# Ten units of an input projection as Strassen products in a hybrid decoder layer

## The chip, the core and the metric

The kernel runs on one core of one Trainium2 chip. The metric is device time in microseconds (us) of one launch. Five engines with a queue of their own work side by side: TensorE (PE) does matmuls out of SBUF into PSUM, VectorE (DVE) and ScalarE (ACT) do elementwise work, GpSimd (POOL) and SyncE (SP) here mostly issue DMAs. They meet on semaphores.

## What is computed

One decoder layer in fp32 for a prompt of 256 tokens and 8 samples of 8 tokens, 320 tokens in all. The part that the change touches is the first projection and its gates:

```
u = rmsnorm(x, norm1, NORM_EPS) @ w_in
qa, ka, va, qb, kb, vb, g_low, r_b, g_a, g_b = jnp.split(u, offsets, axis=-1)
...
ob = rmsnorm(ob, gla_norm, NORM_EPS).reshape(*x.shape[:-1], B_WIDTH) * jax.nn.silu(r_b)
merged = jax.nn.sigmoid(g_a) * (oa @ w_a) + jax.nn.sigmoid(g_b) * (ob @ w_b)
h = x + merged @ w_o
return h + moe(rmsnorm(h, norm2, NORM_EPS), w_router, b_router, w1, b1, w2, b2)
```

oa is sliding-window attention with a sink per head, ob gated linear attention (GLA) in chunks. r_b has 512 columns, g_a and g_b 1024 each; each column is a sum over 1024 model dimensions. The MoE has 32 experts, whose fp32 weights are most of the 440 MB that the kernel reads.

## The kernel before

**Memory.** `ring` is 20 slots of 2048 fp32 per partition (1 MB each). In the first part its slots hold weight units, small operands and results by name: `region_g` (slots 14 to 17) rbT, rsT, gaT and gbT, `late` (4, 5) the cached keys and values and the attention scores, `low` (0 to 3) the GLA operands and states. Later five rooms of four slots take expert weights as they come free. `xnT` holds the normed input transposed, 8 blocks of 128 dimensions by 320 tokens.

**Projection.** w_in is read in units of 256 columns, 15 of them (`W_UNITS`); six ring slots take them in turn (`load_unit`, L378), each loaded again when the unit in it is used up. `project(n)` (L639 to L691) forms tile n of `TILE_ORDER` in PSUM bank n % 3: first k, v, q and the GLA operands (tiles 0 to 15), then four r_b, eight g_a and eight g_b tiles (16 to 35). Each of these twenty is 8 matmuls of a 128x128 weight block with 320 token columns (L689), and a unit makes two tiles. ACT copies every tile out of its bank (`evacuate`, L1338); g_b tiles go through a sigmoid on the way (L1368), r_b and g_a through one later (`gates_early`, L1414).

**Order around the change.** It is written out by hand. PE runs its twenty tiles as s = 0 to 19 and does, behind tile s, the steps of the table `between`: for attention step t of 0 to 4 `scores(t)` (L719), then `turn_probs(t)` (transposes, L743), then `attend(t)` (L756); from s = 12 on the GLA steps `decays`, `turn_keys` (L792), `state_steps(w)` (L800), `sample_reads` and `gla_out`. Among them: s = 4 has turn_probs(0) and scores(1), s = 5 attend(0), s = 6 turn_probs(1) and scores(2), s = 15 state_steps(0) and turn_keys(1), s = 16 state_steps(1) and turn_keys(2), s = 17 state_steps(2) and the prompt's gla_out. ACT has the like table `after`: gla_prep, gla_exps, the exponentials `exps(t)` (L1398), the copies `probs(t)`. DVE's order is a straight list: `softmax_max(t)` (L1705 to L1718) waits for scores(t); `softmax_norm(t)` (L1729 to L1731) waits for exps(t) and releases turn_probs(t); `attended(t)` (L1738) copies attend(t) out. `gla_operands` (L1797 to L1811) stands between softmax_max(1) and attended(0). `mask_keys(t)` (L1765, L1768) waits for turn_keys(t) and releases a later state_steps; `step_states(w)` (L1781 to L1787) takes state_steps(w) out of PSUM. Each engine does its list in order, so what stands behind a waiting instruction waits too.

**After the tiles** PE does `branch` (L906): eight groups of matmuls oa @ w_a, eight ob @ w_b, DVE merging them with the gates. Then `project_h` (merged @ w_o), the router, and the experts.

**SP's order.** Units, then w_a (when tile 29 is done), w_b (after attend(4)), w_o (after all tiles), x again, then expert weights, room by room, each waiting for the event that frees its slots.

**POOL** clears pads, issues the small loads and the stores of new keys and values (L577, L579) and the loads of b1 (L583).

Of the kernel before, what the change touches and what calls it, by code (L numbers as in the profile page):

```python
# [54 lines left out]
FIRST_SLOT, STREAM_SLOTS = 6, 6  # L55
# [6 lines left out]
    + [("vb", t) for t in range(3)] + [("rb", j) for j in range(4)] \  # L62
    + [("ga", j) for j in range(8)] + [("gb", j) for j in range(8)]
FIRST_RB = 16
# [19 lines left out]
def unit_done(m):  # L84

    last = [("va", 2), ("q", 3), ("q", 3), ("qb", 1), ("kb", 1), ("vb", 2), ("vb", 2)]
    return tiles_done(*last[m]) if m < len(last) else FIRST_RB + 2 * (m - 6)

# [71 lines left out]
def layer(nc: bass.Bass, x_prompt, x_sample, cache_k, cache_v, state_gla, norm1, w_in, q_norm, k_norm,  # L160
          sinks, w_gk, b_gk, gla_norm, w_a, w_b, w_o, norm2, w_router, b_router, w1, b1, w2, b2, consts,
          y_prompt, y_sample, k_prompt, v_prompt, s_prompt, k_sample, v_sample, s_sample):
    with ExitStack() as ctx:
# [134 lines left out]
        unit_in = [sem(f"unit_in{m}") for m in range(STREAM_SLOTS)]  # L298
# [6 lines left out]
        pj_ready, pj_freed = sem("pj_ready"), sem("pj_freed")  # L305
        sq_ready, var_ready, qk_rstd, qk_done = (sem(n) for n in ("sq_ready", "var_ready", "qk_rstd", "qk_done"))
# [32 lines left out]
        def slot_of(m):  # L339
            return FIRST_SLOT + m % STREAM_SLOTS  # L340

        def unit(m):
            return ring[:, slot_of(m), :].rearrange("p (k c) -> p k c", k=KD)

# [28 lines left out]
        def _(sp):  # L373
# [4 lines left out]
            def load_unit(m):  # L378
                c = W_UNITS[m]
                sp.dma_start(unit(m), w_in[0, :, c:c + UNIT].rearrange("(k p) c -> p k c", p=P)  # L380
                             ).then_inc(unit_in[m % STREAM_SLOTS], 16)

            for m in range(STREAM_SLOTS):
# [3 lines left out]
            for m in range(STREAM_SLOTS, NU):  # L387
                sp.wait_ge(pj_ready, unit_done(m - STREAM_SLOTS))
                load_unit(m)
                if m == STREAM_SLOTS + 2:  # L390
# [3 lines left out]
            sp.wait_ge(pj_ready, unit_done(13))  # L394
            for g in range(KVH):
                sp.dma_start(wa_sb[HD * g:HD * g + HD, :, :],
                             w_a[0, 256 * g:256 * g + 256, :].rearrange("(j d) c -> d j c", d=HD)).then_inc(wa_in, 16)
            sp.wait_ge(n_ready, use(N_USES, "attend4"))
            sp.dma_start(wb_sb, w_b[0].rearrange("(h v) c -> v h c", v=GDV)).then_inc(wb_in, 16)
            sp.wait_ge(pj_ready, len(TILE_ORDER))  # L400
# [56 lines left out]
            load_half(1, 0)  # L457
            load_half(2, 1)
# [79 lines left out]
        def _(pool):  # L538
# [37 lines left out]
            pool.wait_ge(n_freed, use(N_USES, "keys"))  # L576
            pool.dma_start(k_prompt[0, 0].rearrange("w g d -> w (g d)"), kTok[:, 0, :]).then_inc(stores, 16)  # L577
            for b in range(NSEQ):
                pool.dma_start(k_sample[0, b, P - TSEQ:P].rearrange("w g d -> w (g d)"),  # L579
                               kTok[TSEQ * b:TSEQ * b + TSEQ, 1, :]).then_inc(stores, 16)  # L580

            for g in range(4):
                pool.dma_start(sig_flat.rearrange("p (e x) -> p e x", e=EXPERTS)[:, 8 * g:8 * g + 8, :],  # L583
                               b1[0, 8 * g:8 * g + 8, :].rearrange("e (p x) -> p e x", p=P)).then_inc(b1_in, 16)
# [10 lines left out]
        def _(pe):  # L595
# [38 lines left out]
            def need_unit(m):  # L634
                if m >= unit_at[0]:
                    pe.wait_ge(unit_in[m % STREAM_SLOTS], 16 * (m // STREAM_SLOTS + 1))
                    unit_at[0] = m + 1

            def project(n):  # L639
# [43 lines left out]
                m = {"k": 0, "qb": 3, "kb": 4, "rb": 7, "ga": 9, "gb": 13}[kind] + j // 2  # L683
# [7 lines left out]
                mm.then_inc(pj_ready, 1)  # L691

# [174 lines left out]
            for n in range(FIRST_RB):  # L867
# [26 lines left out]
            for s in range(20):  # L894
                project(FIRST_RB + s)
                for step in between.get(s, ()):
                    step()


            def branch(w_sb, operand, m, u):  # L900
                if u < 3:
                    pe.wait_ge(pj_freed, len(TILE_ORDER))
# [7 lines left out]
            pe.wait_ge(wa_in, 32)  # L910
# [393 lines left out]
        def _(act):  # L1304
# [33 lines left out]
            def evacuate(n):  # L1338
# [22 lines left out]
                elif kind == "glow":  # L1361
                    nc.scalar.copy(glT[:, :], ps[:, n % 3, 0:T]).then_inc(pj_freed, 1)
                elif kind == "rb":
# [745 lines left out]
```

## Time and profile before

| what | us |
|---|---|
| three timed runs: median (lowest to highest) | 1196.55 (1196.08 to 1202.88) |
| the profiled execution | 1200.83 |
| its span, first to last instruction | 1198.6 |
| PE busy in the span | 1156.9 |
| DVE, ACT, POOL busy | 325.8, 170.0, 28.2 |

The profile is of one execution. An engine is busy while an instruction of it is in progress; matmuls are pipelined, so the sum of their lengths is more than the time they take, and what a stream of them costs is read from the spacing. Waiting is shown as the idle time before an instruction, with what ended it. One matmul of the code is two instructions of the profile.

### The profile page before, as it was taken

Reading aid. Unit: us, or ns where it says so; the run is one execution under the profiler, and the core shown is the slowest. Engines: PE = TensorE matmul, PEld = TensorE weight load, DVE = VectorE, ACT = ScalarE, POOL = GpSimd, SP = SyncE. Lnnn points to the kernel's source line nnn. Section 1 sums busy time; section 2 is a strip of 40 time slices with the busy share of each in tenths; the row PEclk is TensorE's granted clock in tenths of the full one; section 3 lists DMA queues with packets and bytes.
Section 4 is the critical chain, followed back from the end, with each engine's and each line's share of the span. In section 5 each row is a group of like instructions: output and inputs, shape, how many; then the busy total and the mean of one; then the engine's idle time right before and its main releaser. Section 6 shows DMA issues by size and latency. Waiting matters only on the chain.

```text
span 1198.6 us, 13581 instructions
## 1 busy us (share of the span) xinstructions
PE 1156.9 (97%) x5929; PEld 552.7 (46%) x5929; DVE 325.8 (27%) x675; ACT 170.0 (14%) x310; POOL 28.2 (2%) x53
## 2 busy tenths in 40 slices
PE   9999999999999999999999999999999999899998
PEld 7676677645344343434344343434343434343433
DVE  3405434624223221212223221222221212121222
ACT  2114322013111010111011010101010101010111
POOL 4102000000000000000000000000000000000000
PEclk9999999999999999999999999999999999999999
DMA  9744153975999999999999999999999999999996
GB/s 303 222 129 118 36 141 133 409 330 198 384 421 428 429 435 431 428 434 432 424 433 436 426 433 433 430 431 430 433 426 435 433 426 431 434 429 425 428 428 243
DMA packets 45054, 439.99 MB, mean 367 GB/s; under 512 B 3646, under 2 KB 21408, under 8 KB 29616
## 3 DMA queue, kind: packets, MB, share of 16 engines
q1 hardware_dynamic: 42864, 434.19, 87.2%
q0 software_dynamic: 1888, 4.10, 1.2%
q8 instruction: 49, 0.80, 0.3%
q10 hardware_dynamic: 240, 0.79, 0.2%
q14 instruction: 13, 0.11, 0.0%
HBM read 436.38 MB, written 3.67 MB: 367 GB/s over the span
## 4 chain that ended last, share of the span: by engine, by line
PE 66%; DMA 30%; DVE 1%; issue 1%; ACT 1%; DVEq 0%
DMA ring<-in_w 30%; PE ps L1125 21%; PE ps L1183 13%; PE ps L689 9%; PE ps L1200 4%; PE ps L906 3%; PE ps L1003 3%; PE ps L926 2%; PE ps L679 1%; PE ps L656 1%; PE ps L1140 1%; ACT xnT L1540 1%; PE ps L1011 1%; PE ps L1152 1%; PE ps L930 1%
## 5 line engine op out<-in xcount | busy, mean ns | idle before, releaser
L1125 PE MATMUL ps<-ring,hnT 128*64 128x512 f32 x2032 | 446.9, 596 | 11.3 <-DMA ring<-in_w 10.6
L1125 PEld LDWEIGHTS ps<-ring,hnT 128*64 128x64 f32 x2032 | 142.9, 137 | 299.8 <-issue 279.6
L1183 PE MATMUL ps<-ring,xnT 128*64 128x512 f32 x992 | 222.6, 601 | 17.6 <-DMA ring<-in_w 17.6
L1183 PEld LDWEIGHTS ps<-ring,xnT 128*64 128x64 f32 x992 | 75.7, 138 | 160.2 <-issue 157.4
L2009 DVE TENSOR_TENSOR xnT<-ps,b1T 128x512 f32<-128x512 f32 x32 | 22.1, 692 | 445.2 <-PE ps L1140 445.2
L689 PE MATMUL ps<-xnT,ring 128*128 128x320 f32 x400 | 114.3, 441 | 1.1 <-DVE xnT L1633 1.1
L1527 ACT COPY hnT<-ps 128x1024 f32<-128x1024 f32 x32 | 32.4, 1012 | 516.0 <-PE ps L1125 516.0
L2030 DVE TENSOR_TENSOR acc<-acc,ps 128x1024 f32<-128x1024 f32 x32 | 38.9, 1218 | 210.1 <-PE ps L1200 210.1
L689 PEld LDWEIGHTS ps<-xnT,ring 128*128 128x128 f32 x400 | 75.5, 192 | 33.8 <-issue 3.0
L1200 PE MATMUL ps<-xnT,cst 128*128 128x512 f32 (+3 forms) x192 | 79.3, 617 | 1.5
L1003 PE MATMUL ps<-cst,region 128*128 128x128 f32 x512 | 63.2, 282 | 0.7 <-issue 0.7
L1003 PEld LDWEIGHTS ps<-cst,region 128*128 128x128 f32 x512 | 59.8, 195 | 2.7 <-issue 0.9
L1539 ACT COPY xnT<-ps 64x512 f32<-64x512 f32 x31 | 17.9, 578 | 245.7 <-PE ps L1183 245.7
L1200 PEld LDWEIGHTS ps<-xnT,cst 128*128 128x128 f32 (+3 forms) x192 | 24.9, 170 | 44.6 <-issue 40.1
L1140 PEld LDWEIGHTS ps<-cst,hnT 128*128 128x128 f32 x256 | 33.3, 210 | 25.9 <-issue 25.2
L1140 PE MATMUL ps<-cst,hnT 128*128 128x128 f32 x256 | 39.3, 297 | 0.6 <-ACT hnT L1527 0.6
L926 PE MATMUL ps<-ring,xnT 128*128 128x512 f32 x64 | 29.8, 603 | 0.0
L2001 DVE TENSOR_TENSOR hnT<-ps,n_cols 128x512 f32<-128x512 f32 x32 | 22.0, 688 | 15.9 <-PE ps L1003 15.9
L1533 ACT ACTIVATE sig<-xnT 128x512 f32<-128x512 f32 x32 | 20.2, 630 | 27.4 <-DVE xnT L2013 27.4
L1988 DVE TENSOR_SCALAR cst<-cst,place,gates 128x64 f32<-128x64 f32 (+1 forms) x96 | 22.6, 303 | 0.0
L2020 DVE SCALAR_TENSOR_TENSOR hnT<-hnT,xnT 128x512 f32<-128x512 f32 x32 | 22.2, 693 | 1.1
L2025 DVE TENSOR_TENSOR xnT<-hnT,sig 128x512 f32<-128x512 f32 x32 | 22.1, 692 | 1.1
(291 smaller groups left out, 666.4 us busy)
## 6 DMA issues: line engine op xcount, KB each, us to landing
ring<-in_w SPq DMA_DIRECT2D x71, 4096.0 KB, 39.7
ring<-in_w SPq DMA_DIRECT2D x46, 2048.0 KB, 17.6
ring<-in_w_in SPq DMA_DIRECT2D x17, 1024.0 KB, 7.7
ring<-in_w_o SPq DMA_DIRECT2D x2, 2048.0 KB, 14.3
ring<-in_w SPq DMA_DIRECT2D x8, 512.0 KB, 23.0
ring<-in_w_a SPq DMA_DIRECT2D x2, 1024.0 KB, 9.6
ring<-in_w_b SPq DMA_DIRECT2D x1, 2048.0 KB, 15.6
ring<-in_w SPq DMA_DIRECT2D x2, 1024.0 KB, 11.6
```

The source lines that it names most:

```text
L689: mm = pe.matmul(ps[:, bank, 0:T], unit(m)[:, k, c:c + P], xnT[:, k, :], start=(k == 0), stop=(k == KD - 1))
L906: mm = pe.matmul(ps[:, u % 3, 0:T], w_sb[:, k, P * m:P * m + P], operand[:, k, :], start=(k == 0), stop=(k == 3))
L926: mm = pe.matmul(ps[:, (XB, VB_)[t] + c, :], xnT[:, k, t0:t0 + r], wo_sb[c][:, k, :], start=(k == 0), stop=(k == KD - 1), skip_group_check ...
L1003: mm = pe.matmul(ps[:, XB + half, P * k:P * k + P], hn[:, t, at:at + P], pick[:, t, :], start=False, stop=last and k == 3, skip_group_chec ...
L1125: mm = pe.matmul(ps[o:o + 64, q // 2, into].rearrange("p (j x) -> p j x", x=4), stationary, columns[:, q], start=(at == 0), stop=(at == KD ...
L1140: mm = pe.transpose(ps[:, 2 + gl, o:o + P], u_sb[:, q, 2 * r + gl:2 * r + gl + 509:4], ident)
L1183: mm = pe.matmul(ps[64 * c:64 * c + 64, 6, :], hT[:, which, order_of(f), :], ring[:, slot, D * (f % 2) + 512 * c:D * (f % 2) + 512 * c + 512],
L1200: mm = pe.matmul(out, lhsT, rhs[half], start=True, stop=True)
L1527: nc.scalar.copy(u_sb[:, :, :], ps[:, 0:2, :]).then_inc(u_copied, 1)
L1988: last = dve.tensor_scalar(gpick[0:r, t, SLOTS * which:SLOTS * (which + 1)], const("slot", r), place[0:r, t, bass.ds(e + which, 1)], gates ...
L2020: dve.scalar_tensor_tensor(lin, lin, 1.0, glu, ALU.add, ALU.mult).then_inc(prod_ready, 1)
L2030: dve.tensor_tensor(acc[:, t, :], acc[:, t, :], ps[:, bank:bank + 2, :].rearrange("p a b -> p (a b)"), ALU.add).then_inc(comb_added, 1)
```

## The change

The ten r_b, g_a and g_b units (u = 0 to 9, 256 columns each) are formed by Strassen's scheme (in Winograd's form). The unit's weights are cut into blocks (i, j): column half i, half j of the 1024 dimensions; `xnT` into blocks of 512 dimensions and 160 tokens. Seven products of half size replace eight: `product(u, i)` is 4 matmuls of a 128x128 block with 160 columns. Three products share a PSUM bank (a group), and ACT copies a group to SBUF at once (`copy_group`). The weight sums of a unit, four additions or subtractions of 512 elements, each waiting for the one before, are done by POOL (`weight_sums`); the four sums of the input blocks once by DVE; and DVE puts the seven products of a unit together in four instructions (`fast_sums`), at places written into its list. The g_b sigmoids move behind that (`gate_b`). Between the fourth and the fifth product of a unit, and behind the seventh, stand the steps that stood behind its two tiles.

The ring is laid out anew: the first seven units have slots of their own, the ten others take slots 8, 6 and 7 in turn, sums go to 9 and 10, the input's sums to 11, products to 19 and the ends of 17 and 18. w_a is loaded later, in two halves, and one expert half waits for the last fast_sums. POOL's stores of keys and loads of b1 now come in pieces between the sums.

```
-            for n in range(FIRST_RB):
+            for n in range(len(TILE_ORDER)):
                 project(n)
...
-            for s in range(20):
-                project(FIRST_RB + s)
-                for step in between.get(s, ()):
+            for u in range(FAST_UNITS):
+                for i in range(4):
+                    product(u, i)
+                for step in between.get(2 * u, ()):
+                    step()
+                for i in range(4, PRODUCTS):
+                    product(u, i)
+                for step in between.get(2 * u + 1, ()):
                     step()
```

PE, a product:

```
+            def product(u, i):
+                at = PRODUCTS * u + i
+                group, part = divmod(at, GROUP_OF)
+                if part == 0:
+                    if group < 3:
+                        pe.wait_ge(pj_freed, len(TILE_ORDER) - 2 + group)
+                    else:
+                        pe.wait_ge(group_copied, group - 2)
...
+                elif i == 2:
+                    pe.wait_ge(halves_ready, 1)
+                    pe.wait_ge(sum_ready, 4 * u + 2)
+                    w, x = sum_w(u, 2), sum_x(2)
...
+                for k in range(4):
+                    mm = pe.matmul(ps[:, (group + 1) % 3, HALF_T * part:HALF_T * part + HALF_T], w[:, k, :], x[:, k, :],
+                                   start=(k == 0), stop=(k == 3), skip_group_check=True)
+                mm.then_inc(product_ready, 1)
```

POOL, the sums of a unit, and what stands between them:

```
+            def weight_sums(u):
+                m = PLAIN_UNITS + u
+                pool.wait_ge(unit_in[m % UNIT_SEMS], 16 * (m // UNIT_SEMS + 1))
+                if u >= 2:
+                    pool.wait_ge(product_ready, PRODUCTS * (u - 1))
...
+                pool.tensor_tensor(sum_w(u, 1), block_w(u, 2, 1), block_w(u, 2, 2), ALU.add).then_inc(sum_ready, 1)
+                pool.wait_ge(sum_ready, 4 * u + 1)
+                pool.tensor_tensor(sum_w(u, 2), sum_w(u, 1), block_w(u, 1, 1), ALU.subtract).then_inc(sum_ready, 1)
...
+            for u in range(FAST_UNITS):
+                weight_sums(u)
+                if u == 2:
+                    store_keys(0, 3)
...
+                elif u in (5, 6):
+                    load_b1(2 * (u - 5), 2 * (u - 4))
```

DVE, the sums of the products, and their places:

```
+            def fast_sums(u):
+                out = fast_out(u)
+                pairs = [out[:, 0:320], out[:, 160:480]]
...
+                dve.wait_ge(group_copied, (PRODUCTS * u + PRODUCTS - 1) // GROUP_OF + 1)
+                link(dve.tensor_tensor(two(pairs[0]), two(products(u, 1, 2)), wide(products(u, 0).unsqueeze(1), [P, 2, HALF_T]), ALU.add))
+                link(dve.tensor_tensor(two(products(u, 0, 2)), two(products(u, 3, 2)), wide(out[:, 160:320].unsqueeze(1), [P, 2, HALF_T]), ALU.add))
+                dve.tensor_tensor(pairs[1], products(u, 5, 2), products(u, 0, 2), ALU.add)
+                dve.tensor_tensor(out[:, 480:640], products(u, 1), products(u, 3), ALU.add).then_inc(out_ready, 1)
...
             for s in range(4):
                 softmax_norm(s)
+                if s == 0:
+                    fast_sums(0)
                 softmax_max(s + 1)
                 if s == 0:
                     gla_operands()
+                fast_sums(s + 1)
                 attended(s)
...
             step_states(1)
+            fast_sums(7)
             mask_keys(2)
             step_states(2)
+            fast_sums(8)
```

DVE between the end of gla_operands and the probabilities of attention step 1; before, the last operand (L1811) is followed by the copy of attend(0) and softmax_norm(1):

```order
L1808 TENSOR_TENSOR region<-ring 64x4x16 x2
L1811 TENSOR_TENSOR ring<-ring 128x640
L1738 COPY hnT<-ps 128x2x128
L1729 TENSOR_TENSOR small<-small 128x4
L1730 RECIPROCAL small<-small 128x4
L1731 TENSOR_TENSOR ring<-ring,small 128x4x128
```

Now, with the lines of the changed kernel (L1974 is the last operand, L1901 the copy, L1892 to L1894 softmax_norm):

```order
L1971 TENSOR_TENSOR region<-ring 64x4x16 x2
L1974 TENSOR_TENSOR ring<-ring 128x640
L1817 TENSOR_TENSOR ring<-ring 128x320
L1818 TENSOR_TENSOR ring<-ring 128x320
L1819 TENSOR_TENSOR ring<-ring 128x320
L1820 TENSOR_TENSOR ring<-ring 128x160
L1901 COPY hnT<-ps 128x2x128
L1892 TENSOR_TENSOR small<-small 128x4
L1893 RECIPROCAL small<-small 128x4
L1894 TENSOR_TENSOR ring<-ring,small 128x4x128
```

The four instructions of fast_sums(1) have come between the operands and softmax_norm(1).

DVE between step_states(1) (L1783, eight instructions) and step_states(2) (L1787), with mask_keys(2) (L1765) between them, before:

```order
L1768 TENSOR_TENSOR region<-ps,cst 128x512
L1783 SCALAR_TENSOR_TENSOR ring<-ring,dec,ps 128x128 x8
L1765 TENSOR_TENSOR region<-ps,cst 64x1024
L1787 SCALAR_TENSOR_TENSOR ring<-acc,dec,ps 128x128 x16
L1832 TENSOR_TENSOR ring<-ring 128x1280
```

Now (L1946 is step_states(1), L1928 mask_keys(2), L1950 step_states(2)):

```order
L1946 SCALAR_TENSOR_TENSOR ring<-ring,dec,ps 128x128 x8
L1817 TENSOR_TENSOR ring<-ring 128x320
L1818 TENSOR_TENSOR ring<-ring 128x320
L1819 TENSOR_TENSOR ring<-ring 128x320
L1820 TENSOR_TENSOR ring<-ring 128x160
L1928 TENSOR_TENSOR region<-ps,cst 64x1024
L1950 SCALAR_TENSOR_TENSOR ring<-acc,dec,ps 128x128 x8
```

fast_sums(7) has come ahead of the mask.

## Rows read from the trace of the kernel before

**Rows 1.** The page: span, chain by engine, and the issues of weight units.

```profile
span 1198.6 us, 13581 instructions
...
PE 66%; DMA 30%; DVE 1%; issue 1%; ACT 1%; DVEq 0%
...
ring<-in_w_in SPq DMA_DIRECT2D x17, 1024.0 KB, 7.7
```

**Rows 2.** Busy time by stage; columns PE, PEld, DVE, ACT, POOL, PEclk, DMA share, GB/s.

```profile
81.00:118.00 37.00, 36.74 (x162) 25.46 (x161) 17.30 (x45) 17.45 (x40) 8.23 (x13) 1.00 0.51 153
118.00:200.00 82.00, 82.00 (x620) 58.94 (x617) 29.31 (x72) 21.19 (x52) 1.91 (x2) 1.00 0.25 71
...
237.00:289.00 52.00, 49.66 (x234) 26.42 (x236) 15.79 (x52) 12.68 (x28) 0.00 (x0) 0.97 0.69 285
289.00:640.00 351.00, 349.73 (x1767) 142.48 (x1765) 88.43 (x181) 39.39 (x58) 0.53 (x1) 1.00 0.99 419
640.00:1173.00 533.00, 503.24 (x2480) 206.73 (x2478) 120.24 (x233) 55.70 (x83) 0.00 (x0) 0.99 1.00 430
```

**Rows 3.** PE's groups by line and shape, 81 to 200 us: the twenty tiles.

```profile
L689 PE MATMUL ps<-xnT,ring 128*128 128x320 f32 x320 | 90.5, 437 | 0.0
```

**Rows 4.** The chain in order of time: start us, us, what.

```profile
49.12 12.92 PE ps L689 x48
...
63.26 14.01 PE ps L656 x64
...
183.18 1.51 PE ps L856 x14
```

**Rows 5.** DVE in order of time, 101 to 117 us.

```profile
106.75 0.76 DVE L1705 SCALAR_TENSOR_TENSOR ring<-ps,cst 128x256 f32<-128x256 f32 x2 [4.32 <-PE ps L727]
...
108.60 0.17 DVE L1797 COPY dec<-ring 128x16 f32<-128x16 f32 x1
...
114.23 0.83 DVE L1811 TENSOR_TENSOR ring<-ring 128x640 f32<-128x640 f32 x1
114.97 0.42 DVE L1738 COPY hnT<-ps 128x256 f32<-128x256 f32 x1
...
115.71 0.69 DVE L1731 TENSOR_TENSOR ring<-ring,small 128x512 f32<-128x512 f32 x1
```

**Rows 6.** Who PE waited for, 81 to 240 us: us, times, longest.

```profile
PE ps L750 <- DVE ring L1731: 0.3, 1, 0.3
```

**Rows 7.** DVE's groups by line and shape, 86 to 117 and 200 to 222 us.

```profile
L1686 DVE TENSOR_TENSOR ring<-ring 128x128 f32<-128x128 f32 x2 | 0.5, 284 | 0.0
...
L1844 DVE TENSOR_TENSOR region<-region,xnT 128x320 f32<-128x320 f32 x4 | 1.8, 442 | 0.0
```

**Rows 8.** DVE, then PE, in order of time, 174 to 182 us.

```profile
176.48 2.53 DVE L1783 SCALAR_TENSOR_TENSOR ring<-ring,dec,ps 128x128 f32<-128x128 f32 x8 [2.58 <-PE ps L812]
178.93 1.21 DVE L1765 TENSOR_TENSOR region<-ps,cst 64x1024 f32<-64x1024 f32 x1
...
176.59 4.47 PE L689 MATMUL ps<-xnT,ring 128*128 128x320 f32 x16
180.99 1.10 PE L812 MATMUL ps<-ring,region 32*64 32x128 f32 x32
```

**Rows 9.** POOL's groups by line and shape, and DVE's slowest group.

```profile
L579 POOL DMA_DIRECT2D out<-hnT x8 | 4.1, 518 | 0.0
...
L543 POOL MEMSET ring<- 128x256 f32 x1 | 0.3, 311 | 0.0
...
L1646 DVE RECIPROCAL acc<-acc 128x320 f32<-128x320 f32 x5 | 10.8, 2153 | 0.2
```

**Rows 10.** The chain late in the kernel, and one stretch by stage.

```profile
677.25 7.10 PE ps L1183 x32
...
736.25 8.72 PE ps L1183 x32
...
736.20:739.60 3.40, 3.35 (x8) 1.13 (x10) 0.00 (x0) 0.00 (x0) 0.00 (x0) 0.51 0.96 414
```

More of the change, by code:

```diff
@@ L386, in _ @@
                     sp.dma_start(cst[:, 2 * P:NCONST], consts[:, 2 * P:NCONST]).then_inc(consts_in, 16)
[L387 to L390, printed above, removed]
+            sp.wait_ge(pj_ready, unit_done(0))
+            load_unit(PLAIN_UNITS - 1)
+            for u, before in enumerate((2, 4, 5)):
+                sp.wait_ge(pj_ready, unit_done(before))
+                load_unit(PLAIN_UNITS + u)
+                if u == 1:
                     sp.wait_ge(qk_done, 5)
@@ new lines, in store_keys, with load_b1 @@
+            def store_keys(first, end):
+                pool.wait_ge(n_freed, use(N_USES, "keys"))
+                if first == 0:
+                    pool.dma_start(k_prompt[0, 0].rearrange("w g d -> w (g d)"), kTok[:, 0, :]).then_inc(stores, 16)
+                for b in range(first, end):
+                    pool.dma_start(k_sample[0, b, P - TSEQ:P].rearrange("w g d -> w (g d)"),
+                                   kTok[TSEQ * b:TSEQ * b + TSEQ, 1, :]).then_inc(stores, 16)
+            def load_b1(first, end):
+                for g in range(first, end):
+                    pool.dma_start(sig_flat.rearrange("p (e x) -> p e x", e=EXPERTS)[:, 8 * g:8 * g + 8, :],
+                                   b1[0, 8 * g:8 * g + 8, :].rearrange("e (p x) -> p e x", p=P)).then_inc(b1_in, 16)
@@ L1360, in evacuate, with copy_group, gate_b @@
                     nc.scalar.copy(kbT[:, j, :], src).then_inc(pj_freed, 1)
-                elif kind == "glow":
+                else:
                     nc.scalar.copy(glT[:, :], ps[:, n % 3, 0:T]).then_inc(pj_freed, 1)
-                elif kind == "rb":
-                    nc.scalar.copy(rbT[:, j, :], src).then_inc(pj_freed, 1)
-                elif kind == "ga":
-                    nc.scalar.copy(gaT[:, j, :], src).then_inc(pj_freed, 1)
-                else:
-                    nc.scalar.activation(gbT[:, j, :], src, ACT.Sigmoid).then_inc(pj_freed, 1)
+            def copy_group(group):
+                first, end = GROUP_OF * group, min(GROUP_OF * group + GROUP_OF, ALL_PRODUCTS)
+                act.wait_ge(product_ready, end)
+                latest = (end - 1) // PRODUCTS
+                if latest >= 2:
+                    act.wait_ge(out_ready, latest - 1)
+                at = first
+                while at < end:
+                    u, i = divmod(at, PRODUCTS)
+                    n = 1
+                    while at + n < end and i + n < PRODUCTS and product_at(u, i + n) == product_at(u, i) + HALF_T * n:
+                        n += 1
+                    part = at - first
+                    out = nc.scalar.copy(products(u, i, n), ps[:, (group + 1) % 3, HALF_T * part:HALF_T * (part + n)])
+                    at += n
+                out.then_inc(group_copied, 1)
+            def gate_b(v):
+                act.wait_ge(out_ready, 7 + v)
+                nc.scalar.activation(gbT[:, 2 * v:2 * v + 2, :], gbT[:, 2 * v:2 * v + 2, :], ACT.Sigmoid).then_inc(gb_ready, 1)
             def root(j):
@@ L1437, in gla_sample_out @@
                 out.then_inc(vw_freed, 1)
-            for n in range(FIRST_RB):
+            for n in range(len(TILE_ORDER)):
                 evacuate(n)
@@ L1821, in _ @@
             mask_decays_prompt()
+            fast_sums(5)
             attended(4)
@@ L1824, in _ @@
             mask_keys(0)
+            fast_sums(6)
             step_states(0)
```

132 lines of the change are left out of this document (101 added, 31 removed).

## Prediction

> **What bounds the kernel now.** I read the page's head and chain first, then the busy time by stage, then PE's chain in order of time, and last what DVE does between two attention steps. The span is 1198.6 us and the chain is PE for 66% of it and DMA for 30% [rows 1]; a reader should ask which of the two rules which stage. The table by stage says it [rows 2]. From 81 to 200 us PE is busy without a gap (36.74 of 37.00, 82.00 of 82.00) while DMA is at 51% and 25%: this stretch, in which the twenty r_b and gate tiles stand between the attention and recurrence steps, is PE's. From 289 us to the end DMA is at 0.99 to 1.00 and 419 to 430 GB/s: the expert weights set the pace. Between them, 237 to 289 us, DMA has only 0.69, so the ring is full and waits for PE to free rooms. A front part that ends x us earlier therefore starts the weight stream x us earlier, and all of x reaches the end. What the change is worth is decided between 81 and 200 us.
>
> **PE work.** The twenty tiles are 320 instructions of 320 columns, 90.5 us as the profile counts them [rows 3]; the count is two per matmul in the code. What one costs is its spacing, from the chain [rows 4]: 48 of them in a row take 12.92 us, 0.2692 each, over three tiles whose waits were already met, so a met wait costs nothing. 64 of 256 columns take 14.01, 0.219 each. 160 columns have no row. Half of 0.2692 is 0.135; a line through 0.219 and 0.2692 gives 0.143, but the 0.219 holds a change of shape. Weight loads set a floor: instructions of only 64 columns behind a full 128x128 load still take 1.51/14 = 0.108. 0.135 is above it, so columns decide; I take 0.136. A product is 4 matmuls, 8 instructions, 1.09 us; a unit of seven is 7.62 against two tiles of 16 x 0.2692 = 4.31, 8.61. That is 1.0 us a unit, 10.0 for ten; with 0.143 it would be 6.0. The steps between stay, so the changes of shape cost what they did.
>
> **What is late next: DVE before turn_probs(1).** PE waits for DVE exactly once in this stretch, 0.3 us, at the transposes of the second attention step [rows 6]. So DVE's chain there had no slack left: from the end of scores(1) it does softmax_max(1) (106.75), gla_operands (108.60 to about 115.1), the copy of attend(0) and softmax_norm(1), ending at 115.71 + 0.69 = 116.40 [rows 5]. The change puts fast_sums(1) into it, behind gla_operands. One fast_sums is three instructions of 320 elements with both inputs in SBUF, 0.44 each, and one of 160, between 0.28 (128 elements) and 0.44, say 0.3 [rows 7]: 1.6 us. fast_sums(0) fits into the idle 4.3 us before 106.75. scores(1) ends 2 x 1.0 us earlier (units 0 and 1; four products, 4.35, cost the same as one tile, 4.31). So turn_probs(1) can start 2.0 - 1.6 = 0.4 us earlier than before, though PE has by then saved more: the first three and a half units yield 0.4 us, and PE idles 0.3 + 1.6 + 1.0 = 2.9 us there, the 1.0 because three products (3.26) stand where a tile (4.31) stood. Behind it the last three products of unit 3 and six units yield 1.05 + 6.0 = 7.05. In the later attention steps fast_sums lies beside ACT's exponentials, and I cost it at nothing; without that cover it is 1.6 us a step.
>
> **And before state_steps(2).** state_steps(2) needs mask_keys(2). Before, DVE did step_states(1) from 176.48 for 2.53 us and then the mask, to 180.14; PE arrived at 180.99, 0.85 late enough [rows 8]. Now fast_sums(7) stands ahead of that mask (+1.6), and PE arrives 1.05 earlier, having three products instead of a tile: 1.6 + 1.05 - 0.85 = 1.8 us lost. fast_sums(8) and (9) lie beside gla_out and the branch matmuls; the extra sigmoids on ACT too. I cost the end at nothing; 0 to 1.6 us if that cover fails.
>
> **POOL.** Forty additions of 512 elements are new; before, POOL did only memsets and DMA issues. A memset of 256 columns takes 0.311 us, so 512 written columns about 0.62; the slowest DVE row, a reciprocal of 320 elements at 2.153, would make 3.4 [rows 9]. I take 1.2, twice the memset, as two inputs are read: 4.8 us a unit, plus up to 4 DMA issues of 0.52. They have from the end of unit u-2 to the third product of unit u, a unit (119/10, less 1) and 2.2 us more: some 13. So as latency they are hidden up to about 2.7 us each. A weight unit lands in 7.7 us [rows 1], requested three units ahead: hidden.
>
> Whether POOL's reads hinder DVE no row shows. About seven of the twelve additions for units 2 to 4 fall where DVE works, with two SBUF inputs, on the chain to turn_probs(1): lower end 0, upper end 7 x 1.2 = 8.4 us. I take the middle, 4.2, since only about half of DVE's instructions there read two SBUF tensors, and a POOL instruction that starts beside another costs nothing.
>
> The Trainium skill speaks against this part of the change: "SBUF — State Buffer", section "Who interferes with whom", has a DVE instruction with two SBUF inputs and a GpSimd instruction that reads SBUF exclude each other for the whole instruction; by it alone the term would lie at its upper end. No row of this trace has the two side by side.
>
> **The clock.** PE's idle time at turn_probs(1) becomes 2.9 + 4.2 = 7.1 us. Late in the kernel waits under 3 us were at times followed by a stretch at half clock: the 32 matmuls at 736.25 took 8.72 us instead of 7.10, and the granted clock was 0.51, the 1.2 GHz level [rows 10]. One such fall: +1.6.
>
> **The sum**, against the profiled execution (1200.83 us, the span and 2.2 around it): -0.4 - 7.05 + 1.8 = -5.65 without POOL's part; + 4.2 + 1.6 gives +0.15. The median of the runs shown, 1196.55, is 4.3 below the profiled execution; the differences are the same for both, so the forecast is 1196.7, in round 1197: no change that counts. About 1% (12 us) is what a measurement of this kernel tells from no change. Its own range is 1193 to 1202.
>
> **Rivals.**
> *POOL does not hinder DVE.* Then -5.65: 1191, without a clock fall, up to 1192.5 with one. For it: DVE's instructions kept their lengths while POOL issued DMAs; against: POOL read no SBUF tensor then. Chance 0.29.
> *Strict turns, slower.* Each POOL addition stands in DVE's way and DVE never goes twice in a row. Then 8.4 at turn_probs(1), and in the next three attention steps four additions fall between softmax_max and softmax_norm: 4 x 1.2 + fast_sums 1.6 + softmax_norm at double width some 1.6 are 8.0. PE's seven products and the attend step take about 8.5 less softmax_max, 1.9 for the width of [rows 5] and about 3 for the double: 5.5 of room, so 2.5 us each, less in the last: 6 in all. -5.65 + 8.4 + 6 + 1.6 = +10.3: 1207. With additions of 1.6 us it is 11.2 + 10.8, +18: 1215; from about 1.3 us on it decides for slower by over 1%. Against: most of POOL's work could as well fall into DVE's idle time, over half of the stretch [rows 2]. Chance 0.25, half of that beyond 1%.
> The price of an addition by the skill alone: "GPSIMD Engine Reference", section "Elementwise — side-by-side cycle accounting", has 4497 ns for 2048 fp32 elements, an estimate of 1.1 us for 512; by it this rival would give 1206.
> *The sums come late.* Above 2.7 us an addition PE waits for sum_ready in each of eight units: at 3.4, 4 x 0.7 = 2.8 us each, +22 and more: 1219. Chance 0.04.
> *All ten us are kept* (DVE is quicker than its rows): 1186.6. The 0.3 us wait speaks against it: no slack to use. Chance 0.03.
>
> **How the numbers follow.** Forecast 0.39, the rivals 0.29, 0.25, 0.04, 0.03. The range must take in POOL-free (1191, with a margin of 3) and strict turns at the price I took (1207, margin 4): 1188 to 1211. That leaves out long additions, late sums and the full gain, some 0.17. Faster by over 1% would be under 1184.6, more than PE can save unless something unseen helps: 0.02. Slower by over 1%, above 1208.5: half of strict turns and late sums, 0.15. The same: 0.83.
>
> **What would show it.** Products at 0.136 us spacing, 7.6 us a unit, show the first step right. PE's wait for DVE at turn_probs(1) should grow from 0.3 to between 3 and 11 us: at 3 POOL is harmless, at 7 my middle holds, above 10 with further waits of 2 us at turn_probs(2) to (4) it is strict turns. A wait of about 1.8 us at state_steps(2) should be new. DVE's two-input instructions of 0.44 and 0.83 us should show longer ones among them where POOL adds; POOL additions of 1.2 us each. I am wrong if PE waits for sum_ready or group_copied, if the products' spacing is above 0.145, or if the weight stream does not move with the end of the front part.

## The result, and the profile after

The changed kernel takes 1206.64 us (median of 18 executions, 1203.4 to 1210.6) against 1198.44 for the kernel before, measured beside it: a ratio of 1.0066, 95% interval 1.0054 to 1.0078. The forecast was 1197. The measured time lies inside the range given, 9.6 us above the forecast, and 8.2 us above the kernel before.

The page of the changed kernel's profile, its head, the chain by engine and two groups:

```profile
span 1207.1 us, 14208 instructions
...
PE 62%; DMA 30%; DVE 4%; ACT 2%; issue 1%; DVEq 0%
...
L806 PE MATMUL ps<-xnT,ring 128*128 128x160 f32 x240 | 36.9, 303 | 2.2 <-ACT ring L1500 2.2
L806 PE MATMUL ps<-ring 128*128 128x160 f32 x240 | 37.3, 307 | 0.0
```

Against [rows 1] the chain has lost 4% of PE and gained 3% of DVE and 1% of ACT. The same two stages as in [rows 2], and the last one:

```profile
81.00:118.00 37.00, 32.86 (x238) 30.64 (x238) 22.97 (x41) 17.69 (x41) 20.93 (x19) 1.00 0.38 117
118.00:200.00 82.00, 72.67 (x659) 66.31 (x660) 50.08 (x104) 23.26 (x56) 32.50 (x27) 0.92 0.38 107
...
640.00:1180.00 540.00, 511.75 (x2512) 208.83 (x2510) 122.50 (x236) 54.72 (x82) 0.00 (x0) 0.99 1.00 430
```

PE was busy for 118.74 of these 119.00 us before; now it is for 105.53, so 13.5 us of waiting stand in it, and from 118 us on its mean granted clock is 0.92. The weight stream still runs at 430 GB/s and a DMA share of 1.00 at the end, so what the front loses reaches the end. Who PE waits for from 78 to 210 us (us in all, times, longest), where [rows 6] had 0.3:

```profile
PE ps L867 <- DVE ring L1894: 7.5, 2, 6.8
PE ps L806 <- ACT ring L1500: 2.2, 1, 2.2
PE ps L929 <- DVE region L1928: 2.0, 1, 2.0
PE ps L866 <- DVE ring L1894: 1.8, 2, 1.5
```

The first row is turn_probs(0), 0.8, and turn_probs(1), 6.8; the last is turn_probs(2) and (3); L929 is state_steps(2), L1928 the mask that it waits for. The second was not on my list, but among my signs of being wrong: a product (L806) waits for ACT's copy of a group (group_copied). PE's timeline shows where, ACT's shows why, and DVE's shows where ACT's 4.23 us come from; POOL's timeline beside them has two of its additions:

```profile
102.66 1.35 PE L806 MATMUL ps<-xnT,ring 128*128 128x160 f32 x8 [2.18 <-ACT ring L1500]
...
123.58 1.09 PE L867 MATMUL ps<-cst,ring 128*128 128x128 f32 x4 [6.76 <-DVE ring L1894]
```

```profile
99.49 0.74 ACT L1521 ACTIVATE ring<-ring 128x640 f32<-128x640 f32 x1 [4.23 <-DVE ring L1849]
...
102.01 0.60 ACT L1500 COPY ring<-ps 128x160 f32<-128x160 f32 x2
```

```profile
92.70 1.47 DVE L1841 SCALAR_TENSOR_TENSOR ring<-ring 128x640 f32<-128x640 f32 x1 [4.98 <-ACT ring L1517]
94.20 3.52 DVE L1843 TENSOR_TENSOR_SCAN ring<-cst,ring 128x320 f32<-128x320 f32 x2
...
105.19 1.63 DVE L1894 TENSOR_TENSOR ring<-ring,small 128x512 f32<-128x512 f32 x1
```

```profile
93.56 1.73 POOL L642 TENSOR_TENSOR ring<-ring 128x512 f32<-128x512 f32 x1
95.38 1.67 POOL L644 TENSOR_TENSOR ring<-ring 128x512 f32<-128x512 f32 x1
```

L1894 is softmax_norm: 0.69 us in [rows 5], here 1.63. The two scans take 3.52, where the kernel before has this group:

```profile
L1680 DVE TENSOR_TENSOR_SCAN ring<-cst,ring 128x320 f32<-128x320 f32 x2 | 1.5, 813 | 0.0
```

POOL's additions grow as well, from 1.27 where DVE is idle to 1.73: the two engines hinder each other, one instruction at a time. ACT stands in gla_exps for DVE's decays, and the group copies stand in its queue behind it.

Last, the clock. Busy time by stretch (columns as in [rows 2]), behind the waits at turn_probs(1) and at state_steps(2):

```profile
123.50:127.50 4.00, 3.92 (x15) 2.79 (x16) 0.77 (x2) 0.59 (x1) 0.00 (x0) 0.50 0.00 0
...
188.40:192.50 4.10, 4.02 (x48) 3.88 (x49) 2.83 (x10) 0.00 (x0) 0.00 (x0) 0.69 0.94 223
192.50:196.00 3.50, 3.50 (x19) 3.50 (x18) 0.95 (x3) 0.00 (x0) 0.00 (x0) 0.50 0.12 23
```

Twice PE runs at 1.2 GHz for some microseconds after it had been idle. The first weight load of the ten units' stretch is at 80.9 us and the first of the branch at 209.3:

```profile
L806 PEld LDWEIGHTS ps<-xnT,ring x240: 186/190/192, 80.9 to 206.3; 128*128 128x128 f32 x120
...
L1028 PEld LDWEIGHTS ps<-hnT,ring x64: 190/190/192, 209.3 to 228.3; 128*128 128x128 f32 x64
```

128.4 us, where the timeline of the kernel before has 80.80 to 199.62, 118.8. This length is the measure of what follows, since it leaves out what happens ahead of the stretch and behind it.

### The profile page after: what moved, and what is told of

It reads as the page before. It is cut to its first block, busy times and chain, and to the rows that moved or that the text cites. A ratio compares the mean times of both kernels' runs of the same rounds, so it can differ in the third digit from the quotient of the medians.

```text
span 1207.1 us, 14208 instructions
## 1 busy us (share of the span) xinstructions
PE 1153.5 (96%) x6169; PEld 572.7 (47%) x6169; DVE 362.3 (30%) x719; ACT 177.4 (15%) x327; POOL 83.7 (7%) x93
## 4 chain that ended last, share of the span: by engine, by line
PE 62%; DMA 30%; DVE 4%; ACT 2%; issue 1%; DVEq 0%
DMA ring<-in_w 30%; PE ps L1247 21%; PE ps L1305 13%; PE ps L1322 4%; PE ps L806 3%; PE ps L1028 3%; PE ps L1125 2%; PE ps L1048 2%; PE ps L773 2%; PE ps L763 1%; PE ps L740 1%; PE ps L1262 1%; ACT xnT L1685 1%; PE ps L1133 1%; PE ps L1052 1%
## 5 line engine op out<-in xcount | busy, mean ns | idle before, releaser
L806 PE MATMUL ps<-xnT,ring 128*128 128x160 f32 x240 | 36.9, 303 | 2.2 <-ACT ring L1500 2.2
L806 PE MATMUL ps<-ring 128*128 128x160 f32 x240 | 37.3, 307 | 0.0
L806 PEld LDWEIGHTS ps<-xnT,ring 128*128 128x128 f32 x240 | 33.5, 190 | 4.5 <-ACT ring L1500 2.8
L806 PEld LDWEIGHTS ps<-ring 128*128 128x128 f32 x240 | 34.3, 194 | 1.5 <-issue 1.2
L773 PE MATMUL ps<-xnT,ring 128*128 128x320 f32 x80 | 23.8, 458 | 1.1 <-DVE xnT L1778 1.1
## 6 DMA issues: line engine op xcount, KB each, us to landing
ring<-in_w_o SPq DMA_DIRECT2D x2, 2048.0 KB, 14.9
```

The lines of the kernel that those rows point to most:

```text
L773: mm = pe.matmul(ps[:, bank, 0:T], unit(m)[:, k, c:c + P], xnT[:, k, :], start=(k == 0), stop=(k == KD - 1))
L806: mm = pe.matmul(ps[:, (group + 1) % 3, HALF_T * part:HALF_T * part + HALF_T], w[:, k, :], x[:, k, :], start=(k == 0), stop=(k == 3), skip ...
```

## The experiments

My theory after this: the products save their 10 us; POOL's additions and those instructions of DVE that need two SBUF operands take turns, which makes DVE late and, through it, ACT; fast_sums at two places makes two of the waits; and PE idling costs a second time through the clock. The rivals: POOL is harmless and only the places count; DVE lacks time as a whole, so a wait that is mended comes back elsewhere; the clock falls for reasons of its own.

### POOL writes, but doesn't read

```
-                pool.tensor_tensor(sum_w(u, 1), block_w(u, 2, 1), block_w(u, 2, 2), ALU.add).then_inc(sum_ready, 1)
+                pool.memset(sum_w(u, 1), 0.0).then_inc(sum_ready, 1)
```

(so for all four sums)

> The changed kernel, but POOL writes the forty weight sums with a memset each (same places, same waits, no SBUF read); the weight sums themselves are left out. Theory (POOL's additions and DVE's instructions with two SBUF inputs take turns): DVE's instructions return to their lengths of before (128x640 with two inputs 0.83 us, scans 0.81), PE's waits for ACT's group copy (2.2), at turn_probs(0) (0.8), (2) (0.4) and (3) (1.7) go, the one at turn_probs(1) falls from 6.9 to about 2.9, and with it the clock fall behind it (2.3): 1206.6 - 2.2 - 0.8 - 0.4 - 1.7 - 4.0 - 2.3 = 1195. Rival (the places of fast_sums and gla_operands in DVE's list make the waits by themselves, POOL is harmless): the wait at turn_probs(1) stays above 6, time 1204 or more.

Measured: 1201.41 us (1190.9 to 1204.5), ratio 0.9995 (0.9967 to 1.0023). Its waits and the two rows of DVE that answer to those above:

```profile
PE ps L867 <- DVE ring L1894: 3.0, 1, 3.0
PE ps L929 <- DVE region L1928: 2.0, 1, 2.0
```

```profile
92.83 0.83 DVE L1841 SCALAR_TENSOR_TENSOR ring<-ring 128x640 f32<-128x640 f32 x1 [4.98 <-ACT ring L1517]
93.69 1.54 DVE L1843 TENSOR_TENSOR_SCAN ring<-cst,ring 128x320 f32<-128x320 f32 x2
```

The waits are those of the theory to 0.1 us, the wait behind ACT among those that went (the 6.9, 0.4 and 1.7 of the expectation are 6.8, 0.3 and 1.5 in the trace): 8.5 of the 13.5 us come from POOL's additions. A memset is also shorter, 0.53 us against 1.27, so that POOL is done before the scans start; but what stands beside one keeps its length (the 0.83 above, a softmax_norm of 128x1024 with 1.23, which in the changed kernel took 2.16), and no instruction of DVE grows beside one in this trace. The time is 6 us above what I expected, and its twelve executions fall in two groups, four of 1190.9 to 1192.5 (mean clock 0.993 to 0.995) and eight of 1201.0 to 1204.5 (0.984 to 0.991). The profiled one is of the second and has PE at a mean clock of 0.96 from 100 to 140 us and 0.95 from 140 to 210: the clock did not stay up as the expectation had it, and both falls come behind the waits of 3.0 and 2.0 us that were left.

### POOL reads one operand

```
-                pool.tensor_tensor(sum_w(u, 1), block_w(u, 2, 1), block_w(u, 2, 2), ALU.add).then_inc(sum_ready, 1)
+                pool.tensor_copy(sum_w(u, 1), block_w(u, 2, 1)).then_inc(sum_ready, 1)
```

> The changed kernel, but each of POOL's forty sums is a copy of its first operand (128x512, one SBUF input); the second operand of each weight sum is left out. Theory one (any POOL instruction that reads SBUF takes turns with DVE's two-input ones): DVE's rows stay long (128x640 at 1.5 us and more), the wait at turn_probs(1) stays at 5 us or more, time 1204 to 1207. Theory two (only POOL instructions with two SBUF inputs do): as with the written-only sums, a wait of 3.0 us at turn_probs(1), none at turn_probs(0), (2) and (3), time as there.

Measured: 1196.87 us (1191.1 to 1203.4), ratio 0.9989 (0.9965 to 1.0014). Waits of 3.5 us at turn_probs(1) and 2.0 at state_steps(2), no others in this stretch. One of POOL's four groups:

```profile
L640 POOL COPY ring<-ring 128x512 f32<-128x512 f32 x10 | 6.4, 642 | 0.6
```

By time and waits it looks like theory two, but DVE's rows say otherwise: some still grow beside a copy (softmax_norm of 128x1024 from 1.23 to 1.49 us, the fourth instruction of fast_sums from 0.32 to 0.73). One read is enough to hinder; a copy only holds for 0.64 us instead of 1.27. My theory one had the mechanism and a wrong price (it wanted 5 us at turn_probs(1) and 1204), and the run does not speak for theory two. How much of the 8.5 us comes from an addition's reads and how much from its length is not separated: copies, hardly longer than the memsets, bring 0.5 of it back.

### The same additions in the kernel before

```
+            def extra_sums(u):
+                pool.wait_ge(pads_ready, 6)
+                pool.wait_ge(xnT_ready, KD)
+                pool.wait_ge(pj_ready, 16 + 2 * (u - 1))
+                for i in range(4):
...
+                    pool.tensor_tensor(scratch[:, 2048:2560].rearrange("p (k c) -> p k c", k=4), xnT[:, 0:4, 0:P],
+                                       xnT[:, 4:8, 0:P], ALU.add).then_inc(extra_done, 1)
```

> The kernel before, with no Strassen product in it, to which twenty POOL additions of 128x512 with two SBUF inputs are added, paced as in the changed kernel (four behind each of tiles 17, 19, 21, 23 and 25); nobody uses their sum. Theory (turns): eight or so of them fall on DVE's chain ahead of turn_probs(1), whose wait grows from 0.3 to 5 us or more, and half a microsecond to two come at later attention steps: 1198.4 + 5 to 10 = 1203 to 1208. Rival (POOL's reads do not hinder DVE): 1198.4, and DVE's two-input instructions keep 0.83 us.

Measured: 1204.94 us (1202.8 to 1209.0), ratio 1.0048 (1.0033 to 1.0063), 6.3 us above the kernel before. PE's waits, 78 to 210 us, and one of DVE's rows:

```profile
PE ps L776 <- DVE ring L1758: 5.0, 2, 3.2
PE ps L775 <- DVE ring L1758: 0.3, 1, 0.3
```

```profile
93.95 3.51 DVE L1707 TENSOR_TENSOR_SCAN ring<-cst,ring 128x320 f32<-128x320 f32 x2
```

No product of Strassen's is in this kernel, and the scans are as long as in the changed one. Twenty additions that nobody uses (with POOL's stores in pieces between them, as in the change) cost 6 us: in the profile 5.0 of new waiting (1.8 at turn_probs(0), 3.2 at turn_probs(1)) and 1.6 of clock. The wait at turn_probs(1) alone is less than the 5 that I expected for it; the rest stands at turn_probs(0) already.

### The mask ahead of fast_sums(7)

```
-            fast_sums(7)
             mask_keys(2)
+            fast_sums(7)
```

> The changed kernel with fast_sums(7) behind mask_keys(2) in DVE's list instead of ahead of it. Theory (each place of fast_sums costs what PE idles, and a clock fall behind it costs again): the wait of 2.0 us at state_steps(2) goes, and the half clock that followed in gla_out and state_steps(3) (3.3 us) with it: 1206.6 - 2.0 - 3.3 = 1201.3. Rival one (the clock falls for another reason than this wait): only the wait goes, 1204.6. Rival two (the sums are only late elsewhere, step_states(2) now has 1.6 us in front of it): 1206.

Measured: 1201.1 us (1200.2 to 1203.5), ratio 1.0022 (1.0012 to 1.0032), 5.5 us less than the changed kernel for two lines exchanged. The wait at state_steps(2) is 0.3, and the granted clock from 140 to 210 us is 1.00. The theory's 1201.3 holds; a wait of 2.0 us cost more than twice its length. Ahead of this place the two profiles come to the same, though divided otherwise: waits and clock together are 15.1 us in the changed kernel and 14.9 here, where a stretch at half clock behind the wait of 2.2 us took up the 0.8 at turn_probs(0) and 1.0 of the wait at turn_probs(1).

### gla_operands in pieces

```
                 if s == 0:
                     fast_sums(0)
+                else:
+                    gla_operands(s - 1)
                 softmax_max(s + 1)
-                if s == 0:
-                    gla_operands()
                 fast_sums(s + 1)
```

(gla_operands(i) does the i-th part of the work)

> The changed kernel with gla_operands cut into three pieces that stand behind softmax_norm(1), (2) and (3) in DVE's list, where DVE waits for the next scores, instead of in one piece between softmax_max(1) and softmax_norm(1). Theory (turn_probs(1) is late because DVE's list has no slack ahead of it, of which gla_operands takes over 6.5 us): the wait of 6.9 us at turn_probs(1) falls below 1 and the clock stays up there (2.3), while 0 to 2 us come back at turn_probs(2) to (4): 1206.6 - 6.5 - 2.3 + 1 = 1199. Rival (DVE lacks time as a whole between 100 and 160 us, so the wait only moves to turn_probs(2) to (4)): waits there grow by 4 us or more, time 1204 or more.

Measured: 1207.28 us (1199.5 to 1211.2), ratio 1.0066 (1.0048 to 1.0084): nothing won. My theory falls here, and the rival's time holds: the wait at turn_probs(1) is gone, but turn_probs(2), (3) and (4) wait 3.1, 1.2 and 1.0. That is 3.5 us more than they had, a little less than the 4 that the rival asked for. All waits together fell from 13.5 to 9.5 us, and in the profile the clock took 3.5 of that back.

```profile
PE ps L866 <- DVE ring L1894: 4.3, 2, 3.1
PE ps L806 <- ACT ring L1500: 2.2, 1, 2.2
PE ps L929 <- DVE region L1928: 2.0, 1, 2.0
PE ps L869 <- DVE ring L1894: 1.0, 1, 1.0
```

DVE's timeline ahead of turn_probs(2), and POOL's at the same time:

```profile
121.27 1.20 DVE L1880 TENSOR_SCALAR small<-small 128x4 f32<-128x4 f32 x1
...
122.97 1.45 DVE L1818 TENSOR_TENSOR ring<-ring 128x320 f32<-128x320 f32 x1
124.45 1.44 DVE L1819 TENSOR_TENSOR ring<-ring 128x320 f32<-128x320 f32 x1
125.81 1.38 DVE L1820 TENSOR_TENSOR ring<-ring 128x160 f32<-128x160 f32 x1
```

```profile
122.52 1.54 POOL L640 TENSOR_TENSOR ring<-ring 128x512 f32<-128x512 f32 x1
124.14 1.40 POOL L642 TENSOR_TENSOR ring<-ring 128x512 f32<-128x512 f32 x1
125.62 1.39 POOL L644 TENSOR_TENSOR ring<-ring 128x512 f32<-128x512 f32 x1
```

This is what turns look like: the three instructions of fast_sums, 0.49, 0.49 and 0.32 us by themselves, wait out one addition each. POOL has some 5.3 us of additions to do for each unit (four of 1.27 and the gaps between them), and they now meet fast_sums and softmax_norm.

### All places mended, then a gate on POOL

The first kernel takes both edits above and moves softmax_max(0) ahead of the decays in DVE's list, exps(0) and gla_exps on ACT:

```
+            softmax_max(0)
             dve.wait_ge(lsp_ready, 1)
...
-                1: [gla_exps],
-                2: [lambda: exps(0)],
+                1: [lambda: exps(0)],
+                3: [gla_exps],
```

> The changed kernel with all places mended, the sums left whole: fast_sums(7) behind mask_keys(2); gla_operands in three pieces behind softmax_norm(1) to (3); softmax_max(0) ahead of the GLA decays in DVE's list, so that turn_probs(0) doesn't wait for them; on ACT exps(0) behind the copies of s = 1 and gla_exps behind those of s = 3, so that no group copy stands behind the wait for the decays. Theory (the waits come from the order of DVE's list and ACT's, and each idle of 2 us or more is followed by a stretch at half clock): waits at the product behind ACT, at turn_probs(0) and at state_steps(2) go, that at turn_probs(1) falls from 6.9 to 1 or less, 3 us at most stay at turn_probs(2) to (4): 1206.6 - 2.2 - 0.8 - 2.0 - 6 + 1 - 3 to 6 of clock = 1191 to 1194. Rival (DVE and POOL together lack time on the port that they share, 5.3 us of additions and some 4.5 of DVE's two-input work in each unit of 10.8 us): waits of 5 us or more stay in sum, wherever they stand, time 1198 or more.

The second adds one wait on POOL:

```
                 if u >= 2:
                     pool.wait_ge(product_ready, PRODUCTS * (u - 1))
+                if 3 <= u <= 7:
+                    pool.wait_ge(p_ready, u - 2)
```

> As the run with all places mended, and besides POOL begins the sums of units 3 to 7 only when softmax_norm of the attention step two and a half units earlier is done (one more wait on POOL), so that its additions fall beside the transposes, scores and softmax_max, in which DVE mostly reads PSUM or waits, and no longer beside fast_sums and softmax_norm. Theory (turns cost only where a two-input instruction of DVE stands beside an addition on the path): waits at turn_probs(1) to (4) under 1 us each, 2 us less in sum than without the gate, 1188 to 1191. Rival (the additions come too late for the products of the next unit): PE waits for the sums, 2 us or more a unit, time 1198 or more.

Measured: 1195.97 us (1194.5 to 1199.1, ratio 0.9971, 0.9958 to 0.9984) for the first, and 1186.85 us (four executions, 1185.7 to 1189.3, ratio 0.9901, 0.9881 to 0.9921) for the second. Without the gate the waits at turn_probs(1) to (4) are 2.9, 1.9, 1.5 and 1.0. So the theory missed, with its 1 us or less at turn_probs(1) and its 1191 to 1194; the rival's sum of 5 us or more holds, though not its time. The second kernel has the waits that its theory asked for and is 1.2 us below its range. With the gate PE's waits from 78 to 210 us, POOL's gated addition, and the ends of the stretch are:

```profile
PE ps L931 <- DVE region L1931: 0.3, 1, 0.3
```

```profile
109.84 1.93 POOL L640 TENSOR_TENSOR ring<-ring 128x512 f32<-128x512 f32 x1 [2.22 <-DVE ring L1897]
```

```profile
L808 PEld LDWEIGHTS ps<-xnT,ring x240: 186/190/193, 78.9 to 184.4; 128*128 128x128 f32 x120
...
L1030 PEld LDWEIGHTS ps<-hnT,ring x64: 189/190/192, 187.5 to 206.4; 128*128 128x128 f32 x64
```

POOL idles 2.22 us for softmax_norm and then adds beside transposes, scores and softmax_max. Turns are still taken (the two scans have 2.49 us instead of 1.54, an operand of 128x640 1.89 instead of 0.83), but PE no longer waits for them. The stretch takes 108.6 us, 10.2 less than before, PE is busy in it but for 0.3 us and the clock stays at 1.00 from 78 to 210 us. This kernel beats both: 12.3 us below the kernel before, measured beside it, and 19.8 below the changed one.

### The gate alone, and the gate without the pieces

The first is the changed kernel with only the gate; the second is the best kernel with gla_operands whole again.

> The changed kernel with the gate on POOL alone (the sums of units 3 to 7 begin when softmax_norm of the step two and a half units earlier is done), all other places as the change has them. Theory (the gate only takes the additions away from fast_sums and softmax_norm; the waits that the order of the lists makes stay): waits at turn_probs(2) and (3) go (0.4 and 1.7), at turn_probs(0) too (0.8), 2.2 behind ACT's copy and 2.0 at state_steps(2) stay, at turn_probs(1) 4.5 to 6 stay, with both clock falls: 1206.6 - 0.4 - 1.7 - 0.8 - 1.5 = 1202. Rival one (the gate is nearly all that is needed): 1195 or less. Rival two (no turn on the path is moved): 1205 or more.

> The kernel with all places mended and the gate, but gla_operands in one piece again, between softmax_max(1) and softmax_norm(1). Theory (what DVE has to do ahead of turn_probs(1) must fit beside a unit of 10.8 us; 6.5 us of gla_operands do not fit): a wait of 4 to 5 us at turn_probs(1) and a half clock behind it, no other wait over 0.5: 1186.9 + 4.5 + 3 = 1194. Rival (with the gate the order of DVE's list no longer matters): 1187 to 1189, no wait over 1 us.

Measured: 1205.13 us (1197.7 to 1211.5, ratio 1.005, 1.0028 to 1.0072) and 1194.25 us (1193.1 to 1195.1, ratio 0.9962, 0.9948 to 0.9976). With the gate alone the waits at turn_probs(0), (2) and (3) are gone as the theory had it, and 4.4 at turn_probs(1), 2.2 behind ACT and 2.0 at state_steps(2) stay; 1.1 at attend(0) is new, PE waiting there for ACT's copy of the probabilities. The profiled execution took 1198.0 and is one of four at 1197.7 to 1199.4; the other eight took 1204.5 to 1211.5, so that the median lies where rival two had it, and not at the theory's 1202. The second comes within 0.3 us of its forecast, with one wait above half a microsecond, at turn_probs(1):

```profile
PE ps L869 <- DVE ring L1897: 4.6, 1, 4.6
```

So neither part does it alone: the gate takes the turns off the path, and the order of the lists makes room for what DVE has to do anyway. Without both the median is 1206.6, with the gate 1205.1, with the order 1196.0, with both 1186.9.

### A control

```
                 softmax_norm(s)
+                if s:
+                    gla_operands(s - 1)
                 softmax_max(s + 1)
-                if s == 0:
-                    gla_operands()
```

(and the moves of softmax_max(0), exps(0) and gla_exps)

> A control: the kernel before with the same places mended as far as it has them (softmax_max(0) ahead of the decays, exps(0) and gla_exps moved on ACT, gla_operands in three pieces), without any product of Strassen's. Theory (before, PE lost only 0.3 us in this stretch, so the order has nothing to give there): 1198, within 1 us of the kernel before. Rival (the better order is worth its microseconds by itself, and what the mended kernels gain is not the products'): 1194 or less.

Measured: 1198.04 us (1195.6 to 1203.0), ratio 0.9997 (0.9984 to 1.001). In the kernel before, the better order gives nothing that can be measured. So the best kernel's gain needs the products: 10.2 of its 12.3 us lie in their stretch. Where the other 2 us come from no run settles, since the control has none of the change's other parts; in the profiles the best kernel's stretch also begins 1.9 us earlier, with a granted clock of 1.00 from 0 to 20 us where the kernel before has 0.91.

### One sum for nine kernels

Take the stretch of the best kernel without its one wait, 108.3 us, add PE's waits between 78 and 210 us, and add the time that the clock takes: one less the mean granted clock, times the length, from 100 to 140 and from 140 to 210 us.

| kernel | first load to branch | waits | clock | 108.3 + both |
|---|---|---|---|---|
| best (ordered, gated) | 108.6 | 0.3 | 0 | 108.6 |
| gated, operands whole | 115.0 | 4.9 | 1.6 | 114.8 |
| one operand read | 115.7 | 5.5 | 1.6 | 115.4 |
| written only | 118.3 | 5.0 | 5.1 | 118.4 |
| ordered | 118.3 | 7.6 | 1.6 | 117.5 |
| gate only | 120.1 | 9.7 | 1.6 | 119.6 |
| mask first | 122.9 | 10.0 | 5.2 | 123.5 |
| changed | 128.4 | 13.5 | 7.1 | 128.9 |
| operands spread | 128.4 | 9.5 | 10.6 | 128.4 |

The sum holds within 0.8 us each time. In the changed kernel 13.5 us of waits and 7.1 of clock stand against the 10 us that the products save. Each row is one execution: that of gate only is 7 us faster than its kernel's median and that of ordered 3 slower, so the rows explain executions and not medians.

## Why the prediction came out as it did

**The products (10.0 us): right.** The best kernel's stretch is 10.2 us shorter than that of the kernel before. In the changed kernel products begin 1.09 us apart, 0.136 an instruction, the spacing that I took:

```profile
109.36 1.25 PE L806 MATMUL ps<-xnT,ring 128*128 128x160 f32 x8
110.45 1.25 PE L806 MATMUL ps<-acc,ring 128*128 128x160 f32 x8
```

**fast_sums(1) ahead of turn_probs(1) (2.9 us) and fast_sums(7) ahead of the mask (1.8): right.** With POOL only writing, these two waits stand alone, at 3.0 and 2.0.

**POOL's addition (1.2 us): right,** 1.26 to 1.28 where DVE is idle. The estimate from the Trainium skill's "GPSIMD Engine Reference", 1.1, was a little low; the trace's 1.27 decides. The time that the prediction gives by this estimate, 1206, is about 1205 when its own sum is worked out with 1.1.

**POOL's hindrance (4.2, the middle of 0 and 8.4): the step that failed.** Whoever reads only the wait at turn_probs(1) finds 6.8 less 3.0, 3.8, and would call the middle right. But the same turns made 2.2 us behind ACT, 0.8 at turn_probs(0) and 1.8 at turn_probs(2) and (3), 8.5 in all, twice my term and as much as the upper end of my bounds, which I had meant for turn_probs(1) alone. The reason that I gave for the middle, that only half of DVE's instructions there have two SBUF inputs and that an addition beside another instruction costs nothing, asked how long DVE's chain to one place becomes. The first half of it was wrong as well, since instructions with one SBUF input were held up too (last section). And I left out who else waits for DVE: the decays of the GLA part are DVE's too, ACT stands in gla_exps until they are done, and the group copies, which the change itself had added, stand behind gla_exps. The Trainium skill, "SBUF — State Buffer", section "Who interferes with whom", has the two engines shut each other out for whole instructions, and a GpSimd instruction that only writes not; both agree with the runs here (a softmax_norm of 128x1024 took 2.16 us beside additions, 1.23 beside memsets).

**fast_sums in the later attention steps, costed at nothing beside ACT's exponentials: wrong in this kernel.** The cover is long enough for fast_sums without turns (1.8 us) and not with them. The chain of the changed kernel (start us, us, what) has fast_sums(3), 3.7 us in all, and a softmax_norm of 2.17, 1.23 without turns, ahead of turn_probs(3), where PE waits 1.5:

```profile
142.63 1.44 DVE ring L1819
144.07 1.31 DVE ring L1820
...
146.82 2.17 DVE ring L1894
```

In the kernel with spread operands fast_sums(2) takes 4.7. With POOL writing, or gated, there is no wait there, so the cover itself was judged rightly.

**The clock (one fall, 1.6): too small.** By rows it is 7.1 us, a fall at each of two waits. The second came behind the 2.0 us at state_steps(2), a wait that I had in the sum without a fall.

**The sum.** I wrote +0.15 for the profiled execution; its span grew by 8.5. The branch starts 9.7 us later, the first expert matmul 8.4: from branch to experts the kernel before takes 1.3 us longer, with a mean clock of 0.97 in [rows 2] where this kernel has 1.00 (245 to 300 us). The rival of strict turns had named 1207, but with other parts: 8.4 at turn_probs(1), where 3.8 was the turns' share, 6 in the next three attention steps, where PE waited 1.8, nothing behind ACT, and 1.6 of clock. Its time was right by luck and its list was not. And that the measured time lies in my range is owed to this rival, for which the range was made so wide, and not to the sum that gave 1197.

## What to carry to other kernels

Work that is given to an idle engine is not free if its reads hold up a busy one's instructions, as POOL's additions made two scans take 3.5 us instead of 1.5: look for its instructions beside the other's, let it start on an event of the other engine behind which that engine waits or reads elsewhere, and mind each queue that waits for the hindered one. A matmul engine that was busy without a gap often pays for an idle stretch a second time, at half clock (14 of 19 waits here), so waits that look too small to matter are worth mending, and what a change is worth may show only when the last of them is gone.

## What the runs showed of the hardware that was not expected

- **An addition on POOL also holds up small instructions of DVE with a single SBUF input.** In the kernel with spread operands a TENSOR_SCALAR of 128x4 took 1.20 us instead of 0.17 (the row above), and a COPY of 128x16 out of SBUF 1.24 instead of 0.17. Instructions of DVE that read PSUM beside one SBUF operand, reductions and reciprocals kept their lengths beside additions (128x4 reciprocals 0.18, 128x128 updates out of PSUM 0.35). That copies and tensor_scalar can contend with GpSimd stands in the same section of the Trainium skill's "SBUF — State Buffer".
- **Short waits were followed by half clock, but not each time.** In the stretch from 78 to 210 us of the traces taken, PE waited between 1.9 and 6.8 us nineteen times; 14 of these waits were followed by PE at 1.2 GHz, five (2.2, 2.2, 2.0, 2.0 and 2.9) were not, and no wait of 1.8 us or less was. No fall in this stretch came without such a wait. One wait of 2.0 us, in the kernel with spread operands, was followed by 7.0 us lost. Executions of one kernel differ too: with the gate alone they take 1197.7 to 1199.4 us at a mean clock of 0.991 to 0.993, or 1204.5 to 1211.5 at 0.981 to 0.989; with hardly a wait left, in the best kernel, 1185.7 to 1189.3. What decides it in one execution stays open.
- In the kernel whose additions only write, the two groups lie about 10 us apart, while the profiled execution shows 5.1 us of clock in this stretch; only one execution of it was profiled, so the rest is not accounted for.
